# Turning the expert products round: weights as the stationary operand, in plain single precision

## The reference

```python
gate, idx = lax.top_k(aff.T, cap)
xe = hf[idx]
he = jax.nn.silu(jnp.einsum('ecd,edf->ecf', xe, w_e1)) * jnp.einsum('ecd,edf->ecf', xe, w_e3)
ye = jnp.einsum('ecf,efd->ecd', he, w_e2) * gate[..., None].astype(h.dtype)
out = jnp.zeros_like(hf).at[idx.reshape(-1)].add(ye.reshape(-1, d))
```

## Time and profile before

| | us |
|---|---|
| median of 3 runs | 2879.96 |
| lowest and highest | 2878.84, 2883.97 |
| the profiled execution | 2884.09 |
| its span, first to last instruction | 2882.3 |

### The profile page before, as it was taken

The page is one execution under the profiler, slowest core; times in us unless marked ns, Lnnn a source line. Parts: engine busy times, 40 slices in busy tenths (PEclk is TensorE's granted clock), DMA queues, the critical chain, the costliest instruction groups (busy, mean ns, idle before and its releaser), DMA issues. The chain is left out here.

```text
span 2882.3 us, 55324 instructions
## 1 busy us (share of the span) xinstructions
PE 2545.9 (88%) x23444; PEld 1914.9 (66%) x23444; DVE 1778.1 (62%) x1920; ACT 1247.9 (43%) x1275; POOL 445.5 (15%) x438
## 2 busy tenths in 40 slices
PE   5999995888888888888789679999999999999993
PEld 4999893777777777788544446666666666666661
DVE  2344213745736547454114578888888888888894
ACT  2212212443534424433100156666666666666671
POOL 0000000431412314314002400111110101110111
PEclk8999995998989989989799789999999999999996
DMA  8453321000000000000451199999999999999983
GB/s 316 148 196 102 119 79 54 17 11 19 12 23 19 11 18 22 11 3 10 156 198 42 64 385 373 344 372 340 367 349 371 339 372 341 372 338 372 343 323 117
DMA packets 246218, 537.95 MB, mean 187 GB/s; under 512 B 13254, under 2 KB 53926, under 8 KB 245752
## 3 DMA queue, kind: packets, MB, share of 16 engines
q1 hardware_dynamic: 242936, 524.39, 49.3%
q0 software_dynamic: 3072, 10.49, 1.6%
HBM read 504.15 MB, written 30.70 MB: 186 GB/s over the span
## 5 line engine op out<-in xcount | busy, mean ns | idle before, releaser
L1724 DVE TENSOR_TENSOR w_lo<-w_raw,w_hi 128x4096 fp32r<-128x4096 f32 x192 | 866.9, 4521 | 116.7 <-ACT w_hi L1564 116.6
L1564 ACT ACTIVATE w_hi<-w_raw 128x4096 fp32r<-128x4096 f32 x192 | 695.6, 3623 | 126.7 <-PE ps_y L1663 87.8
L1661 PE MATMUL ps_h<-w_hi,xT_hi 128*80 128x512 f32 x1024 | 413.1, 403 | 34.7 <-DVE xT_lo L1755 26.8
L1662 PE MATMUL ps_h<-w_lo,xT_hi 128*80 128x512 f32 x1024 | 408.3, 399 | 0.0
L1663 PE MATMUL ps_h<-w_hi,xT_lo 128*80 128x512 f32 x1024 | 407.8, 398 | 0.0
L1661 PEld LDWEIGHTS ps_h<-w_hi,xT_hi 128*80 128x80 f32 x1024 | 154.3, 151 | 119.9 <-DVE xT_lo L1755 25.7
L1661 PE MATMUL ps_y<-w_hi,hiddenT_hi 128*80 128x512 f32 x512 | 204.6, 400 | 14.1 <-DVE hiddenT_lo L1782 14.1
L1663 PEld LDWEIGHTS ps_h<-w_hi,xT_lo 128*80 128x80 f32 x1024 | 154.4, 151 | 87.9 <-issue 4.7
L1662 PEld LDWEIGHTS ps_h<-w_lo,xT_hi 128*80 128x80 f32 x1024 | 154.6, 151 | 81.2 <-issue 4.2
L1662 PE MATMUL ps_y<-w_lo,hiddenT_hi 128*80 128x512 f32 x512 | 201.6, 394 | 0.0
L1663 PE MATMUL ps_y<-w_hi,hiddenT_lo 128*80 128x512 f32 x512 | 201.4, 393 | 0.0
(11 more groups left out here) (282 smaller groups left out, 4045.4 us busy)
## 6 DMA issues: line engine op xcount, KB each, us to landing
w_raw<-in_w_e SPq DMA_DIRECT2D x192, 2048.0 KB, 8.7
w_ada<-in_w_ada SPq DMA_DIRECT2D x6, 4096.0 KB, 18.0
w_in_raw<-in_w_in SPq DMA_DIRECT2D x23, 1024.0 KB, 6.2
rkv_scratch<-projected SPq DMA_DIRECT2D x24, 320.0 KB, 6.4
rkv_T<-rkv_scratch SPq DMA_DIRECT2D x8, 960.0 KB, 5.4
gates_scratch<-projected SPq DMA_DIRECT2D x16, 320.0 KB, 6.6
gate_sb<-gates_scratch SPq DMA_DIRECT2D x8, 640.0 KB, 6.4
x<-in_x_sample SPq DMA_DIRECT2D x8, 512.0 KB, 6.4
```

The lines of the kernel that those rows point to most:

```text
L1564: act.activation(high_of[w][:, :, :], raw[w][s % 2][:, :, :], ACT.Copy).then_inc(s_hi[w], 1)
L1661: pe.matmul(out, x[0][:, k, :], w[0][:, k, ks], start=first, stop=False, skip_group_check=True)
L1662: pe.matmul(out, x[0][:, k, :], w[1][:, k, ks], start=False, stop=False, skip_group_check=True)
L1724: v.tensor_tensor(low_of[w][s % 2][:, :, :], raw[w][s % 2][:, :, :], high_of[w][:, :, :], ALU.subtract).then_inc(s_lo[w], 1)
```

## The change

The kernel after multiplies the other way round. The weights are used as they land, unsplit and in plain single precision, as square blocks of 128x128; they are the stationary operand, and the 80 slots stream. The hidden values come out with the inner features on partitions, which is what the product with w_e2 needs, so `turn` and both splits go. The output comes out turned, with the 1024 channels on partitions in eight tiles of 80 columns, and TensorE turns it back (`turn_y`, eight transposes for each expert).

A round now has four steps of half an expert. The weights come in pieces of four blocks of 128 rows by 1024 columns, 2 MB again, six for each step: w_e1 and w_e3 for the first half of the channels, both for the second half, and two of w_e2, which belong to the step before. Eight buffers are used in turn. One semaphore counts used pieces, and SyncE, ScalarE and VectorE wait on it. The scaling by the gate and the modulation row is now one VectorE instruction on each half of the rows; GpSimd is left with the indirect DMAs.

```diff
-    NST, FK, NR = 2 * FQ, FW // P, NE // 2
+    NR, HF, KQ = NE // 2, 2, 4
+    FH, FK = DE // HF, DE // HF // P
+    NBUF, STEP, ROUND = 8, 6, 24
     W1, W3, W2 = range(3)
+    A, B = slice(0, CAP_L), slice(CAP_L, CAP)
+    KN, PER = DM // P, 4
...
+        raw = [sb(f"w_piece{b}", [P, KQ, DM]) for b in range(NBUF)]
...
+        ps1, ps3, psY = [ctx.enter_context(nc.psum_tensor(n, [P, 1024], F32)) for n in ("ps_h1", "ps_h3", "ps_yT")]
+        psT = ctx.enter_context(nc.psum_tensor("ps_y_rows", [P, 512], F32))
...
+        tile_of = lambda t, n: t[:, n // PER * 512 + n % PER * CAP:n // PER * 512 + (n % PER + 1) * CAP]
...
+        def landed(eng, i, p):
+            b = p % NBUF
+            eng.wait_ge(s_raw[b], 16 * (3 * i + p // NBUF + 1 - (b in (4, 5))))
+        def consumed(eng, i, p):
+            early = isinstance(i, int) and ROUND * i + p < 4
+            eng.wait_ge(s_used, ROUND * i + p + (1 if early else -1))
...
+            def load(i, p):
+                s, n = divmod(p, STEP)
+                if n < 4:
+                    e, hf, w = 2 * i + s // 2, s % 2, (W1, W3)[n % 2]
+                    src = views[w][:, bass.ds(e, 1), n // 2 * KQ:(n // 2 + 1) * KQ, hf * FH:(hf + 1) * FH]
+                else:
+                    e, hf = (2 * i - 1, 1) if s == 0 else (2 * i + (s - 1) // 2, (s - 1) % 2)
+                    f0 = hf * FK + (n - 4) * KQ
+                    src = views[W2][:, bass.ds(e, 1), f0:f0 + KQ, :]
+                sp.dma_start(raw[p % NBUF][:, :, :], src.rearrange("p a k f -> p (a k) f")).then_inc(s_raw[p % NBUF], 16)
...
+                for p in range(ROUND):
+                    if first and p in (4, 5):
+                        continue
+                    if not first or p >= NBUF:
+                        consumed(sp, i, p - NBUF)
                         sp.sem_inc(s_turn, 1)
...
-            def high(w, i, s):
-                act.wait_ge(s_raw[w][s % 2], 16 * (NST // 2 * i + s // 2) + 16)
-                act.activation(high_of[w][:, :, :], raw[w][s % 2][:, :, :], ACT.Copy).then_inc(s_hi[w], 1)
...
+            def sigmoid(i, s):
+                consumed(act, i, STEP * s + 2)
+                act.activation(split(sg), banked(ps1), ACT.Sigmoid).then_inc(s_sg, 1)
...
+                act.activation(split(yT), banked(psY), ACT.Copy).then_inc(s_yc, 1)
...
-                g_.tensor_tensor(ye[j][:, 0:DM], ye[j][:, 0:DM], g2row[:, :], ALU.mult)
...
-            def split_product(out, x, w, k, ks, first, last_):
-                pe.matmul(out, x[0][:, k, :], w[0][:, k, ks], start=first, stop=False, skip_group_check=True)
-                pe.matmul(out, x[0][:, k, :], w[1][:, k, ks], start=False, stop=False, skip_group_check=True)
-                return pe.matmul(out, x[1][:, k, :], w[0][:, k, ks], start=False, stop=last_, skip_group_check=True)
...
+            def hidden(i, s, kh):
+                x = xT[s // 2]
+                if kh == 0 and s % 2 == 0:
+                    pe.wait_ge(s_xt, 4 * i + s + 2)
+                for n, (ps, free) in enumerate(((ps1, s_h1), (ps3, s_hh))):
+                    p = STEP * s + 2 * kh + n
+                    if kh == 0 and (s or not at_zero(i)):
+                        pe.wait_ge(free, 4 * i + s)
+                    landed(pe, i, p)
+                    pe.sem_inc(s_pe_turn, 1)
+                    w = raw[p % NBUF]
+                    for f in range(FK):
+                        for q in range(KQ):
+                            k = KQ * kh + q
+                            last = pe.matmul(tile_of(ps, f), w[:, q, f * P:(f + 1) * P], x[:, k, :], start=(k == 0 and f % PER == 0),
+                                             stop=(k == KD - 1), skip_group_check=True)
+                    last.then_inc(s_used, 1)
             def output(i, s):
+                p = STEP * (s + 1) + 4
+                hf, n = s % 2, 2 * i + s // 2
+                pe.wait_ge(s_hh, 4 * i + s + 1)
+                if hf == 0 and (s or not at_zero(i)):
+                    pe.wait_ge(s_yc, n)
+                for a in range(2):
+                    if s == 3:
+                        landed(pe, i + 1, p - ROUND + a)
+                    else:
+                        landed(pe, i, p + a)
+                    pe.sem_inc(s_pe_turn, 1)
+                    w = raw[(p + a) % NBUF]
+                    for m in range(KN):
+                        for q in range(KQ):
+                            f = KQ * a + q
+                            last = pe.matmul(tile_of(psY, m), w[:, q, m * P:(m + 1) * P], hT[s % 2][:, f, :],
+                                             start=(hf == 0 and f == 0 and m % PER == 0), stop=(hf == 1 and f == FK - 1), skip_group_check=True)
+                    last.then_inc(s_used, 1)
+            def turn_y(i, j, b):
+                n = 2 * i + j
+                if b == 0:
+                    pe.wait_ge(s_yc, n + 1)
+                if b or j or not at_zero(i):
+                    pe.wait_ge(s_ye, 2 * n + b)
+                pe.sem_inc(s_pe_turn, 1)
+                for m in range(PER):
+                    last = pe.transpose(psT[0:CAP, m * P:(m + 1) * P], yT[:, PER * b + m, :], ident[:, :])
+                last.then_inc(s_ytr, 1)
             def body(i, first, last):
-                for s in range(NST):
-                    before = (i, s - 1) if s else None if first else (i - 1, NST - 1)
-                    hidden(W1, i, s)
-                    if before:
-                        turn(*before)
-                    hidden(W3, i, s)
-                    if s == FQ and not last:
-                        slots(i + 1)
+                for s in range(4):
+                    prev = (i, s - 1) if s else None if first else (i - 1, 3)
+                    done = (i, 0) if s == 3 else (i - 1, 1) if s == 1 and not first else None
+                    hidden(i, s, 0)
                     if s < 2:
                         turn_x(i, 2 + s)
-                    if s >= NST - 2 and not last:
-                        turn_x(i + 1, s - NST + 2)
-                    if before:
-                        output(*before)
+                    if s == 2 and not last:
+                        slots(i + 1)
+                    if s == 3 and not last:
+                        turn_x(i + 1, 0)
+                    if done:
+                        turn_y(*done, 0)
+                    hidden(i, s, 1)
+                    if s == 3 and not last:
+                        turn_x(i + 1, 1)
+                    if done:
+                        turn_y(*done, 1)
+                    if prev:
+                        output(*prev)
...
-            def low(w, i, s):
-                v.wait_ge(s_hi[w], NST * i + s + 1)
-                v.tensor_tensor(low_of[w][s % 2][:, :, :], raw[w][s % 2][:, :, :], high_of[w][:, :, :], ALU.subtract).then_inc(s_lo[w], 1)
...
+                v.tensor_copy(xT[j][:, h * KH:(h + 1) * KH, :], psG[:, 0:KH * CAP].rearrange("p (k c) -> p k c", c=CAP)).then_inc(s_xt, 1)
+            def gate_up(i, s):
+                v.wait_ge(s_sg, 4 * i + s + 1)
+                v.tensor_tensor(split(hT[s % 2]), split(sg), banked(ps1), ALU.mult).then_inc(s_h1, 1)
                 v.drain()
+                consumed(v, i, STEP * s + 3)
+                v.tensor_tensor(split(hT[s % 2]), split(hT[s % 2]), banked(ps3), ALU.mult).then_inc(s_hh, 1)
+            def gated(i, j, b):
+                cs = slice(b * 512, (b + 1) * 512)
+                v.wait_ge(s_ytr, 4 * i + 2 * j + b + 1)
+                if b == 0:
+                    if not at_zero(i):
+                        v.wait_ge(s_out[j], 16 * i)
+                    v.tensor_copy(row[j][:, :], gt[j][:, 1:2])
+                v.scalar_tensor_tensor(ye[j][:, cs], psT[0:CAP, :], gt[j][:, 0:1], g2row[:, cs], ALU.mult, ALU.mult).then_inc(s_ye, 1)
```

More of the change, by code:

```diff
@@ L1533, in body @@
-            def body(i, first, last):
-                for s in range(NST):
-                    if not (last and s >= NST - 2):
-                        for w in (W1, W3):
-                            sp.wait_ge(s_used[w], NST * i + s + 1)
-                            load(w, i + (s + 2) // NST, (s + 2) % NST)
-                    if not (first and s == 0) and not (last and s == NST - 1):
-                        sp.wait_ge(s_used[W2], NST * i + s)
-                        sp.sem_inc(s_turn, 1)
-                        load(W2, i + (s + 1) // NST, (s + 1) % NST)
@@ new lines, in consts @@
+            def consts():
+                sp.dma_start(iota[:, :], d["iota_slot"]).then_inc(s_cst, 16)
+                sp.dma_start(tokid[:, :], d["tok_id"]).then_inc(s_cst, 16)
+                for j, rows in enumerate((A, B)):
+                    sp.dma_start(g2row[rows, :], d["mod"][j:j + 1, G2:G2 + DM].to_broadcast([rows.stop - rows.start, DM])).then_inc(s_g2, 16)
+            def body(i, first, last):
+                for p in range(ROUND):
[3 more added lines that the diff above has]
+                        consumed(sp, i, p - NBUF)
```

(45 more changed lines are left out.)

174 lines of the change are left out of this document (38 added, 136 removed).

## The result

The changed kernel takes 4389.23 us in the median (4387.02 to 4391.94, 4 runs), beside 2879.4 us for the kernel before (2869.2 to 2883.97, 4 runs): a ratio of 1.526, 95% interval 1.523 to 1.529. The forecast was 3119 us, its range 3085 to 3185. The sign was right, the size was not: 1270 us more came than was said.

The account below looks back on a forecast made before the run. TensorE's weight loads were taken to bound the expert phase: 1371.3 us of records plus 36 made 1407.3; with 2.5 for the clock, less 1165.2 and 5.4, +239 us, giving 3119 us, range 3085 to 3185.

Parts of the forecast that it names:

- The sign: Whole kernel: the change makes it slower, by 8.3%; slower was given a chance of 0.94.
- the distance of the records: TensorE's expert phase: records start 0.1116 us apart, so 12288 of them take 1371.3 us.
- its clock stood at 0.53 over the first 5 us of products: Start of the expert phase: TensorE comes out of idle at the low clock, which costs 2.5 us.
- Rival C: Expert phase: TensorE's clock at 0.5, records 0.21 us apart, near 4330 us; chance 4%.
- The load bounds a record: TensorE's expert phase: the weight load sets 0.11 us per record and streaming hides behind it; chance 86%.
- covers: Expert phase: work on hidden values and y hides behind products and costs nothing; 48 us if that failed.
- the 1.4 us of the slot products: TensorE's expert phase: slot products take 1.37 us, 7 times, 9.6 us in all.
- The start: Start of the expert phase: x needs one copy per half, so the first product comes 5.4 us sooner.
- The end: From last product to scatter: about 4.5 us, taken as no difference, one us either way.
- Rival B: Expert phase: records pass in under 0.092 us, so DMA binds and the kernel takes some 2830 us; chance 5%.
- Rival D: TensorE's expert phase: gaps per piece, loop end or instruction fetch, 0.4 us per piece making 3196 us; chance 5%.

Follow-up runs that it names:

- experiment 1: The changed kernel with 128 columns streamed behind each weight block in place of 80, the added results not read: 3145.84 us, 1.093 of before.
- experiment 3: The kernel before with eight stretches of matmuls of various shapes put ahead of it, after idle time: 3369.48 us, which includes the stretches and is no comparison.
- experiment 7: The kernel before with nine more stretches of matmuls ahead of it, most warmed by 24 matmuls of 512 columns: 3668.36 us, no comparison.
- experiment 5: The changed kernel with 128 columns streamed (experiment 1) and TensorE's eight rounds written out, without a loop end: 3116.2 us, 1.083 of before.
- experiment 2: The changed kernel with 24 matmuls of 512 columns just ahead of the expert phase's first product, results not read: 4176.76 us, 1.452 of before.
- experiment 8: The kernel before with one VectorE step moved: x's copy put ahead of the split in a round's last step: 2835.81 us, 0.985 of before.
- experiment 4: The kernel before without the split, in plain single precision and the old orientation (x loaded, 512 weight columns streaming): 3058.88 us, 1.064 of before.
- experiment 6: Experiment 1 with 128 columns only in the hidden products of a round's first and third steps, 80 elsewhere: 3144.8 us, 1.092 of before.

## Why the prediction was wrong

**The step that failed** is the distance of the records: "I take 0.1116 us: 12288 x 0.1116 = 1371.3 us". That is the distance at the high clock, and it was taken for the whole phase. Measured were 0.213 us, 2617 us in place of 1371. Under it lies another sentence: "its clock stood at 0.53 over the first 5 us of products; at the low level half the time is lost: 2.5 us". It takes from the old phase that the clock comes up by itself in some 5 us. The old phase came out of idle with 512 streamed columns, the new one with 80, and that does not raise it (experiments 1 and 3).

**Rival C** had the mechanism and the price, near 4330 us for 4389, and was given 4%. It fell short by 59 us: 12288 x 0.003 = 37 are the distance (0.21 for the later 0.213), 27 the transposes and slot products at the low clock (63 for 36), and the earlier start takes 6 off. Two arguments stood against it. "The scan phase ... keeps 1.00": true of that phase, and no evidence for a stream of another shape. "The new stream does more per load than the stretch that fell": right too, since 80 columns hold the clock where 16 lose it (experiment 7, a and b). But both speak of a clock that is held. The phase starts with the low one, and whether 80 columns raise it is another question, which no row of before answered. An unknown that doubles the phase got a weight as though rows had excluded it.

**What held.** The load bounds a record and streaming hides behind it: 16, 80 and 128 columns have one distance, at either clock. The distance at the high clock: 0.1117 in experiment 5, with 1406.7 us for the phase. Counts and covers held (no wait for `hiddenT`, `yT` or `w_piece` within the phase), and so did the 1.4 us of the slot products at the high clock (experiment 2). Experiment 5's 3116.2 us beside the 3119 forecast is the sum as worked out, with two things put in that it lacked, the high clock and rounds without a loop end. That it comes so near is in part luck: its first product came 12.2 us before the old one, at 1663.86, for 5.4 forecast. With the loop ends in, experiment 1 lies 27 us above the forecast.

**The start** was to win 5.4 us and won 11.4. From the first transpose of x to the first product it is 2.82 us for 8.22, the 5.4 of the forecast; the other 6.0 are that the gathered rows came earlier (transposes at 1661.84 for 1667.80). That is no doing of the change: experiment 2, with the changed code up to there, has them at 1667.29, and experiment 8, with the old code, at 1660.67. **The end** was to differ by under one us and does, by 0.8.

**Rival B** is out. The Trainium skill (TensorE: Matmul & The Clock Gate, section on the back-to-back issue gap) gives about 81 ns for a pair at 128 columns; at the high clock the pair here takes 112 ns in the plain type and 113 in the rounded one (34.01 us for 300 in experiment 7). For a load alone the Trainium skill (TensorE: Matmul & The Clock Gate, section LDWEIGHTS) divides the columns by 1.2, an estimated 107 ns for 128, which is nearer the 112.

**Rival D** was dismissed with "loop ends and met waits show none now". Met waits cost nothing, as it said. Loop ends do: the branch took 0.2 us in the kernel before and 3.3 to 6.2 us in the turned ones, and in experiment 1 there are five gaps of TensorE, with the clock lost behind each, 30 us in all (experiment 1 less 5). In the changed kernel itself they cost next to nothing: its TensorE idles 1.0 us in 3 waits on issue; at half the rate the instructions already queued may last over the branch, which was not tried. Rival D had named the fetching of instructions, and the DMA queues bear on it: between 1960 and 2690 us, a stretch with loop ends in both, experiment 1 fetches instructions in 60 transfers, and the kernel before, by its list of queues for the same stretch, in none.

```profile
q8 instruction: 60, 0.98, 0.5%
```

One of these transfers, of 16 KB and some 1 us, lies within each of the five branches (at 2005.67 in the one from 2001.77 to 2008.00). Experiment 5 fetches as often (52 in the same stretch) and has no gap. So the fetch costs where TensorE branches, and not where it goes straight on. It remains an inference that the branch waits for it: experiment 5 took the loop away, not the fetch.

**Where the 1510 us are**, as differences of medians: plain precision in the old orientation +180 (experiment 4), turning the product round +57 (5 less 4), loop ends +30 (1 less 5), the clock +1243 (changed kernel less 1). The parts hold for this order of steps alone: the changed kernel itself loses next to nothing at its loop ends, so that without them the clock's part would be the 30 us larger.

## What to carry to other kernels

Before pricing a long uniform stretch of matmuls, ask two things of the clock: does this shape hold it, and does it raise it from idle? A row of the kernel's other phases answers neither for another shape; where none does, the price of the low clock belongs in the range. And where few columns stream against full 128x128 loads, streaming more of them is free (the load binds) and may bring the clock back: in experiment 6, a third of the records was enough for 1244 us.

## What the runs showed of the hardware

- A TensorE that is busy 999 of 1000 us can stay at 1.2 GHz for the 2680 us of the phase. The Trainium skill (TensorE: Matmul & The Clock Gate, section Part 1: The HAM clock gate) has it that the gate opens by how busy TensorE has been; by the busy share in the profile that does not hold here.
- Raising and holding differ. 80 plain columns on a 128x128 load hold the high clock (89 us alone, 265 us in the kernel) and do not raise it from idle (56 us alone, 2680 in the kernel). 128 columns on 64 rows: held for 45 us, not raised in 56. The rounded type at 128 columns: held for 34, not raised in 56.
- 1.3 to 1.4 us of two-column matmuls between stretches of 80 columns can lose the clock, and these do not bring it back. It happened in the one stretch of experiment 7 and at the second of two such places in experiment 2. What decides between the two places was not tested.
- At the high clock a record with a load of 128x128 costs 0.112 us in plain single precision, where a matmul has two, and 0.113 in the rounded type, where it has one: a plain product in this orientation costs twice a rounded one. With 80 columns loaded it is 22.03 / 300 = 0.073 in the rounded type.
